# Gate products in single pieces, states sent out in halves, constant products at the start, indicators on GpSimd, and earlier loads, in a hybrid decoder layer

## The reference, cut to what matters

```python
xn = rmsnorm(x, norm1_w)
proj = xn @ w_in            # HGRN2 q,f,i,g | RWKV-7 r,k,v,lora | gate_a, gate_b
o_a, s_hgrn_new = hgrn2_chunked(silu(hq), 1 - f, hi, log(f), s_hgrn)
y, s_rwkv_new = rwkv7_scan(r, decay, k, v, kk, a, s_rwkv)
merged = (sigmoid(gate_a) * (o_a @ w_branch_a)
          + sigmoid(gate_b) * (o_b @ w_branch_b))
x = x + merged @ w_out
logits = rmsnorm(x) @ router_w + router_b
# top 4 of 32 experts for each row, softmax over the four
h = x_pad[tok_b] @ w_gu[e] + b_gu[e]
act = glu * sigmoid(1.702 * glu) * (lin + 1.0)
out = act @ w_down[e] + b_down[e]
```

## Time and profile before

| what | us |
|---|---|
| median of 3 runs | 1326.92 (1326.7 to 1327.52) |
| the profiled execution | 1327.32 |
| its span | 1325.6 |
| PE busy in the span | 1288.1 (97%) |
| VectorE, ScalarE, GpSimd busy | 373.8, 242.4, 52.6 |
| moved by DMA | 449.40 MB, mean 339 GB/s |
| granted PE clock, mean | 0.997 of full speed |

### The profile page before, as it was taken

The page is one execution under the profiler, slowest core; times in us unless marked ns, Lnnn a source line. Parts: engine busy times, 40 slices in busy tenths (PEclk is TensorE's granted clock), DMA queues, the critical chain, the costliest instruction groups (busy, mean ns, idle before and its releaser), DMA issues.

```text
span 1325.6 us, 18387 instructions
## 1 busy us (share of the span) xinstructions
PE 1288.1 (97%) x7355; PEld 615.1 (46%) x7355; DVE 373.8 (28%) x1019; ACT 242.4 (18%) x532; POOL 52.6 (4%) x127
## 2 busy tenths in 40 slices
PE   8999999999999999999999999999999999999997
PEld 6778768888754333333333333333333333233333
DVE  3234666554327212121121211212112111211112
ACT  3143343222122101111111111111111101111102
POOL 5000200000050000000000000000000000000000
PEclk9999899999999999999999999999999999999999
DMA  7635426110779999999999999999999999999996
GB/s 232 173 97 190 129 64 198 62 37 33 281 290 375 411 430 427 429 429 428 424 412 429 429 429 430 430 430 430 430 429 430 429 429 430 431 428 429 429 429 278
DMA packets 72720, 449.40 MB, mean 339 GB/s; under 512 B 14388, under 2 KB 43110, under 8 KB 47864
## 3 DMA queue, kind: packets, MB, share of 16 engines
q1 hardware_dynamic: 67090, 445.72, 82.2%
q10 hardware_dynamic: 5574, 2.88, 0.8%
HBM read 443.82 MB, written 4.76 MB: 338 GB/s over the span
## 4 chain that ended last, share of the span: by engine, by line
PE 75%; DMA 18%; DVE 4%; ACT 2%; issue 1%; ACTq 0%; SPq 0%; DVEq 0%
PE bank L1254 24%; PE bank L1274 13%; PE bank L553 8%; DMA ring<-in_expert_w_gu_dram 7%; PE bank L1162 5%; DMA arena<-in_expert_w_gu_dram 5%; PE bank L1193 4%; PE bank L657 3%; DMA extra<-in_expert_w_down_dram 3%; PE bank L1064 2%; DMA extra<-in_expert_w_gu_dram 2%; PE bank L1038 2%; PE bank L931 2%; ACT arena L1400 1%; PE bank L1169 1%; PE bank L914 1%
## 5 line engine op out<-in xcount | busy, mean ns | idle before, releaser
L1254 PE MATMUL bank<-arena 128*64 128x512 f32 x960 | 216.6, 594 | 1.0 <-DMA arena<-in_expert_w_gu_dram 1.0
L1400 ACT ACTIVATE arena<-bank 128x512 f32<-128x512 f32 (+6 forms) x232 | 115.5, 516 | 494.3 <-PE bank L1274 195.9
L1254 PE MATMUL bank<-ring,arena 128*64 128x512 f32 x848 | 189.6, 594 | 3.5 <-DMA ring<-in_expert_w_gu_dram 3.5
L1400 ACT ACTIVATE arena<-arena 128x256 f32<-128x256 f32 (+7 forms) x124 | 69.0, 565 | 470.9 <-DVE arena L2339 463.8
L2339 DVE TENSOR_SCALAR arena<-bank 128x256 f32<-128x256 f32 x64 | 27.0, 422 | 379.2 <-PE bank L1254 379.2
L1254 PEld LDWEIGHTS bank<-arena 128*64 128x64 f32 x960 | 67.2, 137 | 134.5 <-issue 116.9
L553 PE MATMUL bank<-arena,ring 128*128 128x288 f32 (+1 forms) x464 | 118.8, 417 | 0.5 <-ACT arena L1400 0.5
L1254 PEld LDWEIGHTS bank<-ring,arena 128*64 128x64 f32 x848 | 59.7, 137 | 115.4 <-issue 100.0
L2388 DVE COPY arena<-bank 64x512 f32<-64x512 f32 x30 | 20.8, 694 | 319.6 <-PE bank L1274 319.6
L553 PEld LDWEIGHTS bank<-arena,ring 128*128 128x128 f32 x464 | 89.0, 193 | 28.5 <-issue 1.9
L1274 PE MATMUL bank<-arena 128*64 128x512 f32 x448 | 100.6, 595 | 0.0
(11 more groups left out here) (371 smaller groups left out, 1130.7 us busy)
## 6 DMA issues: line engine op xcount, KB each, us to landing
arena<-in_expert_w_gu_dram SPq DMA_DIRECT2D x60, 2048.0 KB, 23.5
ring<-in_expert_w_gu_dram SPq DMA_DIRECT2D x53, 2048.0 KB, 20.6
ring<-in_expert_w_down_dram SPq DMA_DIRECT2D x28, 2048.0 KB, 20.5
arena<-in_expert_w_down_dram SPq DMA_DIRECT2D x28, 2048.0 KB, 26.8
extra<-in_expert_w_gu_dram SPq DMA_DIRECT2D x15, 2048.0 KB, 22.5
ring<-in_w_in_dram SPq DMA_DIRECT2D x23, 1024.0 KB, 5.4
extra<-in_expert_w_down_dram SPq DMA_DIRECT2D x7, 2048.0 KB, 31.7
ring<-in_w_out_dram SPq DMA_DIRECT2D x4, 1024.0 KB, 7.0
```

What stands on the lines that cost most here:

```text
L1254: ins = mm(bank[q % 2][64 * (q // 2):64 * (q // 2) + 64, :], gu_lhs(c), w[:, q * 512:(q + 1) * 512], start=(c == 0), stop=(c == KT - 1), s ...
L1400: return nc.scalar.activation(out, in_, f, **kw)
```

## The change

Single products in place of whole gate tiles ahead of the loop, with the same 56 products in all before it; the store of `s0h` in two halves with a semaphore each, the first waited for by VectorE's mask, the second by ScalarE before its first square evacuation; five constant products before the first transposes and two behind them; `ind` of the first pair by GpSimd, and PE's wait for `gsel_ready` there moved to the second expert; output chunks 6 and 7 ahead of chunk 22, load 3 behind load 2, loads 0 and 4 ahead of the wait for the merge. `btmp` moves from the memory that load 3 now fills. The wait for `rw_in` goes.

```diff
-        btmp = PQ[:, 0:NT]
+        btmp = fm[9][:, 0:NT]
...
-            for n in list(range(N_IN + 4)) + [N_IN + 6, N_IN + 7, N_IN + 4, N_IN + 5]:
+            for n in list(range(EARLY)) + [N_IN + 6, N_IN + 7] + list(range(EARLY, N_IN + 6)):
                 if n == N_IN + 6:
 
-                    sp.wait_ge(S("oa_done"), 9)
+                    sp.wait_ge(S("hg_state"), 8)
+                    sp.wait_ge(S("hg_o_evac"), 3)
                     sp.wait_ge(S("rws_out"), 16 * NB)
                 if n == N_IN + 4:
                     sp.wait_ge(S("rwp_out"), 16)
                     w_load(sp, 0, 2)
+                    w_load(sp, 0, 3)
...
             sp.dma_start(norm_bc, norm2_w.partition_broadcast(P)).then_inc(S("norm_loaded"), 16)
+            w_load(sp, 0, 0)
+            w_load(sp, 0, 4)
             sp.wait_ge(S("merged"), 8)
-            w_load(sp, 0, 0)
             for x in (0, 2, 3):
                 sp.dma_start(braw[NE * x:NE * x + NE, :], expert_b_gu[0]).then_inc(S("braw_loaded"), 16)
-            for s in (3, 5):
-                w_load(sp, 0, s)
-            sp.wait_ge(S("wo_done"), 1)
-            w_load(sp, 0, 4)
+            w_load(sp, 0, 5)
...
+            keep_busy(5, bank[5])
             for t, (o, n) in enumerate(TILES):
...
+            keep_busy(2, bank[5])
             pe.wait_ge(S("xT_evac"), 5)
...
-            gate_m = [KT * WHOLE]
-
-            def fill(u, site):
-
-                while gate_m[0] < gate_products(u, site):
+            gate_m = [0]
+
+            def gate_run(to):
+
+                while gate_m[0] < to:
...
+            def gate(n):
+
+                gate_run(gate_m[0] + n)
+
+            def fill(u, site):
+
+                gate_run(gate_products(u, site))
...
-                gate_tile()
+                gate(3)
                 for G in range(2):
+                    if G:
+                        gate(3)
                     for b in range(NB):
...
-                gate_tile()
+                gate(5)
                 for j in range(3):
+                    if j:
+                        gate(1)
...
+                gate(1)
                 for G in range(2):
                     pe.wait_ge(S("smp_dve"), smp_dve["z"] + 4 + G + 1)
...
-                gate_tile()
+                gate(8)
                 for q in range(4):
...
             smp_scores()
+            gate(2)
             smp_solve()
...
                 if t:
-                    gate_tile()
+                    gate(3)
...
                 if t:
-                    gate_tile()
+                    gate_run(KT * WHOLE)
                 for c in range(4):
                     g = 4 * t + c
                     if g == 0:
                         continue
+                    if t == 0:
+                        gate(1)
...
             def hgrn_sample():
 
+                gate(2)
                 pe.wait_ge(S("hg_o_evac"), 1)
...
+                gate(1)
                 pe.wait_ge(S("hg_state"), 4)
...
                 for g in range(2):
-                    gate_tile()
+                    gate((9, 6)[g])
...
             pe.wait_ge(S("hg_state"), 8)
-            pe.wait_ge(S("rw_in"), 1)
...
-            pe.wait_ge(S("bgu3"), 1)
+            pe.wait_ge(S("bgu3"), 2)
...
                     if c == 6:
-                        if x == 0:
+                        if x == 0 and not first:
                             pe.wait_ge(S("gsel_ready"), i + 1)
...
                     if x == 1:
+                        pe.wait_ge(S("gsel_ready"), i + 1)
                         gt_T()
...
+            def sample_states_out(g):
+
+                act.wait_ge(S("hg_upd"), 4 * g + 4)
+                b = slice(4 * g, 4 * g + 4)
+                act.dma_start(hgrn_s[0, b].rearrange("b h k v -> k (b h) v"),
+                              s0h.rearrange("p (b h v) -> p b h v", b=NB, h=HA)[:, b].rearrange("p b h v -> p (b h) v"))\
+                   .then_inc(S(f"hgrn_out{g}"), 16)
...
+                    sample_states_out(0)
                     keys_evac(2, 1)
-                    act.wait_ge(S("hg_upd"), 8)
-                    act.dma_start(hgrn_s[0].rearrange("b h k v -> k (b h) v"), s0h.rearrange("p (b h v) -> p (b h) v", b=NB, h=HA))\
-                       .then_inc(S("hgrn_out"), 16)
+                    sample_states_out(1)
...
+                if u == 0:
+                    act.wait_ge(S("hgrn_out1"), 16)
                 square_evac(0)
...
-                    dve.wait_ge(S("hgrn_out"), 16)
+                    dve.wait_ge(S("hgrn_out0"), 16)
...
-                    v.tensor_scalar(ind[:, x * SLOTS:(x + 1) * SLOTS], ones[:, 0:SLOTS],
-                                    gselc[:, x * TW + 6:x * TW + 7], None, ALU.mult)
+                    if not (isinstance(i, int) and i == 0):
+                        v.tensor_scalar(ind[:, x * SLOTS:(x + 1) * SLOTS], ones[:, 0:SLOTS],
+                                        gselc[:, x * TW + 6:x * TW + 7], None, ALU.mult)
...
-                i = g.tensor_copy(bgu3[r, :], braw[r, :])
-                step(i, "bgu3" if r.start == 96 else "pool_step")
+                step(g.tensor_copy(bgu3[r, :], braw[r, :]))
+            for x in range(2):
+                step(g.tensor_scalar(ind[:, x * SLOTS:(x + 1) * SLOTS], bcast(pmod, [P, SLOTS]), float(x), None, ALU.is_equal), "bgu3")
```

More of the change, by code:

```diff
@@ L512, in _ @@
             sp.wait_ge(S("shift_out"), 32)
-            sp.wait_ge(S("hgrn_out"), 16)
+            sp.wait_ge(S("hgrn_out0"), 16)
+            sp.wait_ge(S("hgrn_out1"), 16)
             sp.wait_ge(S("rws_out"), 16 * NB)
@@ L534, in _, with keep_busy @@
             done(i, "par_T")
+            def keep_busy(n, b=bank[1]):
+                for _ in range(n):
+                    mm(b[:, 0:P], ident, ones, start=True, stop=True)
+            keep_busy(5, bank[5])
             for t, (o, n) in enumerate(TILES):
@@ L628, in _ @@
                 done(i, "smp_pe")
-            gate_k = [E_BLOCK]
-            def gate_tile():
-                k = gate_k[0]
-                if k >= E_BLOCK + 16:
-                    return
-                gate_k[0] += 1
-                g = k - E_BLOCK
-                n = 15 + g // 2
-                if g % 2 == 0:
-                    chunk_ready(n)
-                bank_free(k)
-                project(k, n, g % 2, NT)
-            gate_m = [KT * WHOLE]
-            def fill(u, site):
-                while gate_m[0] < gate_products(u, site):
+            gate_m = [0]
+            def gate_run(to):
+                while gate_m[0] < to:
                     g, kt = gate_m[0] // KT, gate_m[0] % KT
@@ L1100, in last_logits @@
                 return i
-            def keep_busy(n, b=bank[1]):
-                for _ in range(n):
-                    mm(b[:, 0:P], ident, ones, start=True, stop=True)
             w_out_tile(2, acc(2))
@@ L2057, in _ @@
             dve.wait_ge(S("hg_o"), 2)
-            v.memset(s_all[:, 0:256], 0.0).then_inc(S("rw_in"), 1)
+            v.memset(s_all[:, 0:256], 0.0)
             for g in range(2):
@@ L2271, in _ @@
                                         op0=ALU.add, op1=ALU.mult))
-            dve.wait_ge(S("bgu3"), 1)
+            dve.wait_ge(S("bgu3"), 2)
             for t, (o, rows) in enumerate(TILES):
```

## The result

The changed kernel takes 1321.65 us (median of 6 runs, 1320.5 to 1322.46); the kernel before, on the same chips, 1327.68 (6 runs, 1326.7 to 1330.38). The ratio is 0.9954, 95% interval 0.9943 to 0.9966: 6.0 us faster. I had forecast 1317.6, 9.3 us faster, with a range up to 1321.3. The sign holds, the size was half again too large, and the time lies 0.35 us above the range. Of the 4.05 us between forecast and time, 0.76 is the starting point (1326.92 in the three runs that I had, 1327.68 here), and 3.3 is gain that did not come.

The account below looks back on a forecast made before the run. The end was taken as bound by a DMA stream of expert weights tied to TensorE's slot releases; 0.5 + 4.3 + 2.2 + 0.4 + 1.9 = 9.3 us from 1326.92 gave 1317.6, range 1315.3 to 1321.3.

Parts of the forecast that it names:

- What sets the end: Expert weight stream: PE's gains before 663 us move a slot release and the end, within 3.0 us of slack.
- the stream is the floor: Weight stream: if its pauses are queue latency, the end moves only with load 6; 7.4 us gain, 1319.5, chance 0.10.
- Indicators: First expert: GpSimd makes the indicators and PE's 1.92 us wait for VectorE goes; gain 1.9 us (0.7 to 1.92).
- Sample solve: Samples' solve in the mixer: single gate pieces fill waits and keep the clock up; gain 4.3 us (1.5 to 4.6).
- The rival of a second fall: Samples' solve: the clock falls again, costing 2.5 us of a tile and 0.7 in the solves; 1320.8, chance 0.15.
- HGRN part: HGRN part of the mixer: gate pieces fill PE's waits around state products; gain 2.2 us (1.0 to 2.55).
- Store in halves: Samples' state store: VectorE's first mask waits only for the first half; gain 0.4 us (0 to 0.9).
- The slower rival: First solve: ScalarE's wait for the second half of the store delays the squares; 1331 us, chance 0.03.
- Constants: Kernel start: constant products around the first transposes bring the clock up; gain 0.5 us (-0.3 to 1.0).
- Early loads: Load queue: loads 3, 0 and 4 and two output chunks moved ahead were not waited for; gain 0.

Follow-up runs that it names:

- the three kernels whose release is at 40.8: The kernel before (1327.68 us), the same with the seven constant products alone (1327.18), and the changed kernel with VectorE making the indicators again (1322.18).
- PE held back: The changed kernel with sixteen more constant products behind the ranks, after loads 6 to 9 are released: 1324.79 us.
- the run with whole tiles: The changed kernel with the gate products in the samples' solve as two whole tiles of eight at their old places: 1324.32 us.
- the second kernel without them: The second run of the changed kernel without the five and two constant products around the first transposes: 1322.03 us.

## Why the prediction was wrong, by its own steps

**What sets the end: wrong in one sentence.** That the tail is a stream held by PE's own releases, with pauses where a slot is freed late, held in all 14 profiles. The sentence that failed is that whatever PE gains before 663 moves that release, "and with it the end". The release moved (7.38 us at the first expert, 7.37 at 655.70) and the last bytes with it (7.0), but the kernel's end did not follow in full. Its last 18.7 us hang on one transfer, which lands 4.2 us ahead of the last bytes in the kernel before and 2.7 us ahead in the changed one, so it came only 5.5 us earlier. It was issued 6.58 us earlier (1264.69 for 1271.27) and took 1.07 us longer (36.71 for 35.64). I had taken the end of the stream for the landing that the work behind it waits for. Why the two lie 2.4 to 4.6 us apart, and furthest (4.1 to 4.6) in the three kernels whose release is at 40.8, stays open.

The rival "the stream is the floor" had a chance of 0.10. Its number is near (7.4 us forecast at load 6, 5.25 had there, 5.5 at the last landing), but its mechanism is not what ran: with load 6 in place and PE held back the end moved by 3.2 us, and with load 6 by itself 1.28 us earlier the last landing did not come earlier at all.

**Indicators: forecast 1.9, measured 2.1 at the release (40.8 to 38.7) and 0.5 to 0.8 at the end by medians, no difference within the intervals.** The removed wait and what followed it on PE were right (nothing else was late at 421.51); its worth at the end was the failed step above.

**Sample solve: forecast 4.3, measured 3.8.** From 147.30 to 166.24 are 18.94 us where I had 18.4: the tiny products took 2 x 2.04 and not 3.8, the rest the single pieces cost. The clock stayed at 1.00, as the row of the fall had suggested. The Trainium skill (TensorE: Matmul & The Clock Gate, "HAM oscillation — how this bites in real kernels") puts the fall down to idle time between groups, by which the pieces would have gained nothing at the clock; the measurement decides otherwise: the run with whole tiles brought the fall back with PE 100% busy in every window from 146 to 163. The rival of a second fall is out.

**HGRN part: forecast 2.2, measured 0.86.** The mis-sized part of the term is the cost of 0.5 us for pieces among the groups. I had read 1.5 us of hidden pauses into their 3.38 us for 24 records and let the pieces fill them. Pauses there were: behind the pieces the undivided group takes 2.18 us. But pieces between the groups cost 1.25 us more than the same pieces ahead of them, and the first half of the part loses 1.66 us of its lead. Behind it my numbers held: 2.15 us were gained at the second half, where I had 2.55 less 0.2.

**Store in halves: forecast 0.4, and worth 1.9 at the mask.** In the profile pair the term cannot be seen, since squares and scores moved alike (5.25 and 5.22 us). The run with one store shows why it counts: it would have been issued at 198 and held the mask until 210, so that without the halves PE's gains in this part end at VectorE. The terms aren't additive: undone one by one, the four parts cost 0.52, 4.11, 1.02 and 4.24 us at load 6, 9.9 in all, of the 5.25 that they brought together. I costed each edit on the kernel before, in which the store was barely late, and not on the sum of the others. The slower rival did not come about: ScalarE starts the squares' copies 0.31 us behind PE, not behind a store.

```profile
211.22 0.60 ACT L1407 ACTIVATE ring<-bank 128x512 f32<-128x512 f32 x1 [0.31 <-PE bank L927]
```

**Constants: forecast 0.5, measured 0.55 in this pair of profiles,** 0.08 at the first tile in the kernel before with the constants, 0.52 at load 6 in the second kernel without them, and more in the times (above). This may be why the medians are 6.0 us apart and the profiles 5.45; no run settles it.

**Early loads: 0 and 0.**

So at load 6: 0.55 + 3.81 + 0.86 + 0.03 = 5.25, where I had 0.5 + 4.3 + 2.2 + 0.4 = 7.4; with the indicators 7.4 at the release, where I had 9.3; and 5.5 at the last landing. Half of what is missing was lost in the mixer, mostly in the HGRN part, and half between the release and the last landing. The lower bounds of my terms add up to 1324.0, but I closed the range at 1321.3. That range reached for single terms at their lower ends, but the HGRN term lay below its own lower end of 1.0, and no case of mine had both a smaller gain in the mixer and a loss behind it. That the time missed the range by only 0.35 us says little, since the starting point alone moved by 0.76.

## What to carry to other kernels

When the tail is a stream at full rate, follow three places apart: the release that last held a load back, the stream's last bytes, and the landing that the last work waits for. Here the first two moved together and the third by less. A run that delays the engine on purpose, and one that moves the first load alone, tell which of the two the stream hangs on. Filler products belong in front of a row of narrow products on different columns, not between them, by the one place where two runs compare it. Cost an edit on the kernel with the other edits in it: the halves of a store that was barely late before were what let the earlier products count.

## What the runs showed of the chip that I had not expected

- Products of full width between groups of 32-column products: 0.99 us for a group that takes 0.70 in a row with its like, and 0.65 us for a piece that takes 0.52; 0.63 us for each stretch of groups more.
- The granted clock fell to 0.50 in two different ways: with PE busy, behind 3.90 us of 64x8 products (kernel before and the whole-tile run), and soon after PE had waited 1.66 us in a stretch of light use (one store, 212 to 218). Two groups of 2.04 us of the same products with 1.72 us of full ones between them kept it at 1.00.
- In one execution without constant products the first projection tile took 6.18 us in place of 4.25 with a recorded clock of 1.00 and weight loads of 337 ns, the length they have at 0.50 elsewhere; so a slow start of TensorE need not show in that column.
- The bytes of the weight stream ended 870.5 to 871.0 us behind one release in 14 profiles, while the landing that TensorE waits for last lay anywhere from 866.0 to 868.5 us behind it.
